# Last hidden values split in two parts, and VectorE's products and adds put ahead of weight splits in the small experts

## The reference, cut to what matters

```python
hn = rmsnorm(h, ffn_norm_g)
up = causal_dwconv(hn @ w_up, ffn_conv_w, ffn_conv_b)   # w_up: 2048 x 11264
val, gt = jnp.split(up, 2, axis=-1)
h = h + (jax.nn.silu(gt) * val) @ w_down                 # w_down: 5632 x 2048
x = rmsnorm(h, final_norm_g)                             # end of the first block
...
# second block: norm1 of x (shifted and scaled), attention, norm2, then 16 experts of width 512
def moe_ffn(h, router_w, router_bias, w_gate, w_up, w_down):
    aff = jax.nn.sigmoid(t @ router_w)
    # one of 4 groups of experts for each token, and 2 experts of that group
    ...
    # y = sum over chosen experts of  w_e * (silu(t @ w_gate[e]) * (t @ w_up[e])) @ w_down[e]
```

## Time and profile before

| | |
|---|---|
| median of 3 runs | 2907.25 us |
| the three runs | 2906.62, 2907.25, 2908.99 us |
| the profiled execution | 2910.48 us, its span 2907.6 us |
| TensorE busy in that span | 97% |
| VectorE, ScalarE busy | 76%, 52% |
| mean granted TensorE clock | 0.989 of 2.4 GHz |

### The profile page before, as it was taken

One profiled execution on the slowest core, in us unless ns is written; L12 is line 12 of the kernel. 1 busy time (PEld: TensorE's weight loads), 2 busy tenths in 40 slices (PEclk: granted clock), 3 DMA queues, 4 the chain that ended last, 5 costly groups with the idle time before them and its releaser, 6 DMA issues.

```text
span 2907.6 us, 45616 instructions
## 1 busy us (share of the span) xinstructions
PE 2827.7 (97%) x17842; PEld 2539.5 (87%) x17842; DVE 2197.8 (76%) x2740; ACT 1510.2 (52%) x1723; POOL 158.5 (5%) x228
## 2 busy tenths in 40 slices
PE   9999999999999999999999989999999999999998
PEld 8888888888888899999999989998989999977876
DVE  5644459999876899999999974655765778787786
ACT  5444564445554544444444454556545555556666
POOL 3000010000101000000000020111110000000001
PEclk9999999999999999999999999999999999999999
DMA  7445445555453978888888737444406777778885
GB/s 283 176 157 185 169 157 187 190 190 188 175 220 128 376 312 325 327 329 324 320 328 329 294 120 272 173 168 163 138 19 236 287 263 274 282 279 332 317 326 207
DMA packets 115678, 692.23 MB, mean 238 GB/s; under 512 B 14240, under 2 KB 27792, under 8 KB 34768
## 3 DMA queue, kind: packets, MB, share of 16 engines
q1 hardware_dynamic: 109952, 675.33, 61.5%
q10 hardware_dynamic: 4688, 11.01, 1.2%
q0 software_dynamic: 896, 3.93, 0.4%
HBM read 679.74 MB, written 10.49 MB: 237 GB/s over the span
## 4 chain that ended last, share of the span: by engine, by line
PE 84%; DVE 8%; ACT 4%; issue 2%; DMA 1%; SPq 0%; POOL 0%; DVEq 0%; POOLq 0%; ACTq 0%
PE psT L1310 22%; PE psT L1311 11%; PE psT L1297 6%; PE psT L1298 6%; PE psT L1299 6%; DVE w_lo L2092 4%; PE psT L1419 3%; PE psT L1887 2%; PE psT L1889 2%; PE psT L1888 2%; ACT w_hi L642 2%; PE psT L1898 2%; PE psT L1900 2%; PE psT L1899 2%; PE psT L1421 1%
## 5 line engine op out<-in xcount | busy, mean ns | idle before, releaser
L2092 DVE TENSOR_TENSOR w_lo<-raw,w_hi 128x2048 fp32r<-128x2048 f32 x532 | 1218.5, 2296 | 356.5 <-ACT w_hi L642 351.5
L642 ACT ACTIVATE w_hi<-raw 128x2048 fp32r<-128x2048 f32 x532 | 1013.2, 1910 | 405.4 <-PE psT L1299 130.8
L1310 PE MATMUL psT<-a_both,w_hi 128*128 128x512 f32 x3072 | 1084.2, 398 | 10.1 <-DVE pool L2453 2.9
L1311 PE MATMUL psT<-a_both,w_lo 128*128 128x256 f32 x3072 | 859.0, 280 | 0.0
L1310 PEld LDWEIGHTS psT<-a_both,w_hi 128*128 128x128 f32 x3072 | 577.4, 188 | 149.8 <-issue 8.9
L1311 PEld LDWEIGHTS psT<-a_both,w_lo 128*128 128x128 f32 x3072 | 579.9, 189 | 0.3
L1297 PE MATMUL psT<-a_both,w_hi 128*128 128x256 f32 x784 | 228.6, 292 | 7.7 <-DVE w_lo L2265 2.9
L1298 PE MATMUL psT<-a_both,w_hi 128*128 128x256 f32 x784 | 223.6, 285 | 0.0
L1299 PE MATMUL psT<-a_both,w_lo 128*128 128x256 f32 x784 | 223.6, 285 | 0.0
L2439 DVE CUSTOM_DVE_ANT_0 pool<-pool 128x2048 f32<-128x2048 f32 x96 | 219.2, 2284 | 5.2 <-DVE mod L2447 5.2
L1297 PE MATMUL psT<-h_hi,w_hi 128*128 128x256 f32 x768 | 219.1, 285 | 3.0 <-DVE h_lo L2479 1.7
(11 more groups left out here) (409 smaller groups left out, 4531.1 us busy)
## 6 DMA issues: line engine op xcount, KB each, us to landing
raw<-tiles_dram SPq DMA_DIRECT2D x532, 1024.0 KB, 5.3
pool<-ada_tiles_dram SPq DMA_DIRECT2D x96, 1024.0 KB, 5.0
bias_rows_dram<-pool ACTq DMA_DIRECT2D x1, 8192.0 KB, 56.2
pool<-bias_rows_dram SPq DMA_DIRECT2D x40, 128.0 KB, 4.6
pool<-bias_rows_dram SPq DMA_DIRECT2D x40, 64.0 KB, 4.6
pool<-mem_dram SPq DMA_DIRECT2D x4, 512.0 KB, 8.8
raw<-tiles_dram SPq DMA_DIRECT2D x8, 256.0 KB, 8.3
pool<-x_dram ACTq DMA_DIRECT2D x1, 2048.0 KB, 11.4
```

Source lines behind the costliest of these rows:

```text
L642: nc.scalar.activation(w_hi[:, t.k % SPL, :], raw[:, t.k % RAW, :], ACT.Copy).then_inc(hi_done, 1)
L1310: nc.tensor.matmul(dst.rearrange("p (h s) -> p h s", h=2), wh, a_both[:, :, a, :], start=first, stop=False)
L1311: return nc.tensor.matmul(dst[:, 0:S], wl, a_hi[:, a, :], start=False, stop=last)
L2092: nc.vector.tensor_tensor(w_lo[:, t.k % SPL, :], raw[:, t.k % RAW, :], w_hi[:, t.k % SPL, :].bitcast(F32), ALU.subtract).then_inc(lo_done, 1)
```

## The change

It has three parts. In the **feed-forward tail** the last of the ten loop rounds is written out on ScalarE and VectorE. In its last slot the first three chunks of the hidden values are split as soon as they exist, and the fourth by itself after the last pair; the VectorE split of tile 282 (the third of the last four), which stood in that slot, comes after the fourth chunk. TensorE runs the products of the first of the last four tiles in two parts, chunks 0 to 2 and then chunk 3, without filler ahead of them; the bias rows' product comes after that tile. On VectorE the bias rows' add goes behind the first `add_down`, the gain products of the third group go to the end with those of the fourth, and the split of tile 285 behind them. TensorE's product with the lane goes behind the last chunks 0 to 2.

In the **drained stages** (experts 7 and 11) `expert_hidden` moves from the drain into the last slot of up, ahead of the weight split there; for expert 7 ScalarE's copy of the lower rows moves ahead of its split likewise.

In **gate(9) and gate(13)** `expert_hidden` goes ahead of the first weight split, and the second round's four adds stand together behind the third split, instead of two behind the third and two behind the fourth.

```diff
@@ ScalarE, ffn_groups
-                with act.Fori(0, G1 - 1) as i:
+                def ffn_group(i, b8, last):
                     for n in range(12):
...
                         split(t + k + AHEAD)
+                        if last and n == 11:
+                            act.wait_ge(W["pairs_read"], 4 * G1 + 1)
+                            act.wait_ge(used, (b8 + 7).count())
+                            nc.scalar.activation(h_hi[:, 0:3, :], chunks(HF, 3), ACT.Copy)\
+                                .then_inc(W["last_hidden_hi"], 1)
                         if n // 4 != 1:
                             up_lower(t, k, i + 1, half)
...
+                with act.Fori(0, G1 - 2) as i:
+                    ffn_group(i, Tile(b + 8, i, 12, b + 8), False)
+                ffn_group(G1 - 2, Tile(b + 8 + 12 * (G1 - 2)), True)
                 up_silu(3, G1 - 1, 1)
-                hidden_hi(Tile(b + 12 * G1 - 5), G1 - 1)
+                act.wait_ge(W["pairs_read"], 4 * G1 + 2)
+                nc.scalar.activation(h_hi[:, 3, :], pool[:, HF + 3, :], ACT.Copy).then_inc(W["hidden_hi"], 1)
@@ ScalarE, experts
+                        if k == 3 and e in DRAINED and s == 3:
+                            up_lower_rows(e)
                         split(Tile(up_at(e) + k + AHEAD))
...
                     into = DRAINED[e]
-                    if s == 3:
-                        up_lower_rows(e)
@@ TensorE, ffn_groups
-                idle_products(8)
+                t = Tile(b + 12 * G1 - 4)
+                begin(t)
+                pe.wait_ge(W["last_hidden_lo"], 1)
+                for part in (range(3), range(3, 4)):
+                    if 3 in part:
+                        pe.wait_ge(W["hidden_lo"], G1)
+                    for n in range(4):
+                        for k in part:
+                            ...
+                            nc.tensor.matmul(dst, wh, h_hi[:, k, :], start=k == 0 and n % 2 == 0, stop=False)
+                            nc.tensor.matmul(dst, wh, h_lo[:, k, :], start=False, stop=False)
+                            last = nc.tensor.matmul(dst, wl, h_hi[:, k, :], start=False, stop=k == 3 and n % 2 == 1)
+                last.then_inc(used, 1)
                 pe.wait_ge(L["tables"], 48)
                 nc.tensor.matmul(psP[0:32, :], flat(Q2, 1)[0:32, 0:32], flat(Q2 + 1, 2)[0:32, :], start=True, stop=True)\
                     .then_inc(W["bias_rows"], 1)
-                idle_products(6)
-                pe.wait_ge(W["hidden_lo"], G1)
-                for k in range(4):
+                for k in range(1, 4):
                     down(Tile(b + 12 * G1 - 4 + k))
...
-                run_lane("final", FINAL_LANE, start=False)
+                wait(pe, W["variance_ready"], NORM_AT["final"])
                 for c in range(4):
+                    if c == 3:
+                        pe.wait_ge(W["lanes_added"], 3 * RUN.index("final") + 3)
+                        nc.tensor.matmul(psN, ones[:, :], pool[:, FINAL_LANE, :], start=False, stop=False)
                     run_last("final", c, US)
@@ VectorE, ffn_groups (the round is written out as on ScalarE)
-                            lo(t + n + AHEAD)
+                            if last and n == 11:
+                                dve.wait_ge(W["last_hidden_hi"], 1)
+                                nc.vector.tensor_tensor(h_lo[:, 0:3, :], chunks(HF, 3), h_hi[:, 0:3, :].bitcast(F32),
+                                                        ALU.subtract).then_inc(W["last_hidden_lo"], 1)
+                            else:
+                                lo(t + n + AHEAD)
...
-                hidden_lo(G1 - 1)
+                dve.wait_ge(W["hidden_hi"], G1)
+                nc.vector.tensor_tensor(h_lo[:, 3, :], pool[:, HF + 3, :], h_hi[:, 3, :].bitcast(F32), ALU.subtract)\
+                    .then_inc(W["hidden_lo"], 1)
+                lo(Tile(b + 12 * G1 - 5) + AHEAD)
+                ada_keep(ADA_EACH, G1 - 2)
...
                     if k < 3:
-                        lo(t + AHEAD)
+                        if k < 2:
+                            lo(t + AHEAD)
                         add_down(t + -k, k)
+                        if k == 0:
+                            bias_rows()
+                        if k == 2:
+                            continue
...
+                    for g in (2, 3) if k == 3 else (k,):
+                        ins = nc.vector.tensor_tensor(chunks(PRE + 4 * g, 4), chunks(H + 4 * g, 4), ...)
                 link(ins)
+                lo(Tile(b + 12 * G1 - 2) + AHEAD)
@@ VectorE, experts, stage gate
-                        if k == 0 and before == 0:
+                        early = before == 0 or e - 1 in SCATTERED_IN
+                        if k == 0 and before is not None and early:
                             expert_hidden(e - 1)
...
                         lo(Tile(gate_at(e) + k + AHEAD))
-                        if k == 0 and before:
+                        if k == 0 and before is not None and not early:
                             expert_hidden(e - 1)
-                        if k > 1 and e - 1 in SCATTERED_IN:
-                            round_add(SCATTERED_IN[e - 1], 1, range(2 * k - 4, 2 * k - 2))
+                        if k == 2 and e - 1 in SCATTERED_IN:
+                            round_add(SCATTERED_IN[e - 1], 1, range(4))
@@ VectorE, experts, stage up
+                        if k == 3 and e in DRAINED:
+                            expert_hidden(e)
                         lo(Tile(up_at(e) + k + AHEAD))
@@ VectorE, experts, stage drain
-                    expert_hidden(e)
```

More of the change, by code:

```diff
@@ L2494, in ffn_groups, with ffn_group @@
                 ada_keep(ADA_FIRST)
-                with dve.Fori(0, G1 - 1) as i:
-                    with step.loop(i, 9, G1 - 1):
-                        t = Tile(b + 8, i, 12)
+                def ffn_group(i, t, last):
                         for n in range(12):
```

34 lines of the change are left out of this document (23 added, 11 removed).

## The result

The changed kernel took 2886.86 us (median of 6 runs, 2883.53 to 2889.97) against 2908.12 for the kernel before in the same comparison (6 runs, 2901.89 to 2912.08). The ratio is 0.9923, with a 95% interval of 0.9913 to 0.9933, so the change takes off 22.4 us (19.5 to 25.3); the two medians themselves are 21.3 apart. The forecast was 2881 with a range of 2875 to 2892: side and range held, and the sum of 26.4 was 4.0 us too large and outside that interval. The profiled execution took 2887.1 us for a span of 2885.3, so span against span it is 22.3 shorter.

What follows compares the result with a forecast made beforehand. TensorE's waits and the slow clock behind them were taken to bound the kernel. The terms 7.7 + 4.1 + 0.8 + 7.5 + 6.3 = 26.4 us came off the median of 2907.25, giving 2881, range 2875 to 2892.

Steps and rivals of the forecast that it cites:

- What bounds the kernel: Whole kernel: TensorE carries 84% of the chain; time is won only where it stands still or runs slowly afterwards.
- Part 1a: Feed-forward tail, hidden values in two parts: second down tile starts at 1679.7 instead of 1684.6, 4.9 us won.
- Part 1b: Feed-forward tail, what is late next: fourth down tile waits 1.8 us; GpSimd's last group starts 5.3 us earlier.
- cross-sum: Check of the tail's total: 5.3 + 4.5 less 1.4 and 0.9, said to give 7.7 us within rounding.
- Part 1c: End of the norm: three products follow the lane instead of nine, 4.5 us won; VectorE and GpSimd alternate, root at 1707.5.
- lock rival: Tail: VectorE's three operations go in a row, so the tail gives 5.0 us, time 2884; chance 0.14.
- Part 2: Drained stages: expert 7's wait falls from 3.2 to 0.95, a second is 0.9, gain 4.1 us; expert 11 gains 0.8.
- clock rival: Drain 7: two waits of 0.9 close together still lower the clock, 2.8 us comes back, time 2884; chance 0.13.
- Part 3: Gates 9 and 13: shorter waits and no slow stretch behind them, gains of 7.5 and 6.3 us.
- transfers rival: Experts 8 to 15: without pauses, transfers at 353 GB/s bind and 24 us come back, time 2905; chance 0.06.
- signs that I would be wrong: ScalarE waiting for landings in a row, fourth down tile waiting over 2.4 us, or gates' down products still waiting for L2869.
- part 1: Whole feed-forward tail: root 7.7 us nearer to the last up tile, 34.9 instead of 42.6 behind it; bounds 5.0 to 9.5.

Runs made afterwards that it cites:

- split_only: Kernel before plus only the last hidden values and first down tile in 3 plus 1 parts, bias rows' product behind it; timed once, root 39.6 us behind last up tile.
- lane_back: Kernel before with the whole tail change, but TensorE's lane product ahead of the last four chunks as before; timed once, root 37.2 us behind last up tile.
- adds_first: Changed kernel with the tail's order pushed on: VectorE's second sum and gain products earlier, ScalarE's norm squares ahead of gain squares; 2888.78 us, ratio to before 0.9931.
- drains_only: Kernel before with only the drained stages' part of the change (experts 7 and 11); 2907.86 us, ratio 0.9989.
- early_only: Kernel before with only the hidden values' product ahead of VectorE's first split in gates 9 and 13; timed once, waits of 1.66 gone, those of 3.28 stayed.
- moe_only: Kernel before with only the drains and gates changed, feed-forward tail as before; 2897.86 us, ratio 0.9953.
- filler_only: Kernel before with 24 filler products of TensorE put into each of three waits of 3.2 to 3.3 us; no time given, clock 1.00 in those places.
- adds_only: Kernel before with only the four adds together behind the third split in gates 9 and 13; timed once, L2869 waits gone, those of 1.65 stayed.
- all_orders: Changed kernel with the tail's order pushed on, gate adds ahead of the third split, and a drain split moved behind the lower half; 2891.78 us, ratio to before 0.9933.
- tail_only: Kernel before with only the feed-forward tail's part of the change, experts as before; 2903.22 us, ratio 0.9969.

## Why the prediction was right, and where it was off

**What bounds the kernel**: right. All that TensorE got back were the waits listed in the earlier trace rows, the tail, and the clock.

**Part 1a, 4.9**: the down products start without a gap behind the last up tile, and the gap ahead of chunk 3 is 0.17 (0.35 said). The second down tile starts 7.2 behind the last up tile instead of 12.0, so 4.7 came. `split_only` gives 3.0 at the root for the edit alone, since GpSimd's group then ends last; the prediction didn't claim it alone.

**Part 1b**: the new wait ahead of the fourth down tile is 0.62, not 1.8. The term that I mis-sized is the chain from ScalarE's split of tile 284 to the second add. That add ends at 1695.6, 19.5 behind the last up tile, and I had it 20.4 behind (1693.05 less 1672.65). The wait is 1.2 shorter than said, and the tail gave 9.3 instead of 7.7, inside the bounds of 5.0 to 9.5. The rest of that 1.6, some 0.4, is VectorE's work in the last group, which the prediction ended at 34.9 and which ended at 33.3. The prediction's cross-sum for this part (5.3 + 4.5 less 1.4 and 0.9) makes 7.5 and not 7.7; its timeline carries the 7.7.

**Part 1c**: the alternation of VectorE and GpSimd came as said: GpSimd's adds took 1.59 and 1.59 beside the gain products and the split, where the earlier trace rows have 0.74 alone and 2.79 beside a split. The lane's place is worth 2.2 plus the clock (`lane_back`). The root starts when VectorE's split ends, as said.

Here the page that I had weighed, SBUF — State Buffer in the Trainium skill, section Who interferes with whom, agrees with the trace on the block itself: 1.59, 1.60 and 2.66 for an add of 0.74. The lock rival (5.0, all three in a row) didn't come in after, and in `adds_first`, with more two-input work of VectorE there, the two engines took turns as well; it lost because GpSimd got one add between two of VectorE's instructions.

**Part 2**: the first wait of drain 7 is 0.96 (0.95 said), the second 0.74 (0.9 said), clock 1.00, gain 4.1 as said; drain 11 gives 0.9 (0.8 said). The clock rival is out: two waits of 0.96 and 0.74 close together left it at 1.00, in all five executions that have them. Over 10 runs `drains_only` gives 3.2. With 1.6 of clock, the mean, in place of 2.8 the sum would be 3.7; the runs can't tell it from 4.9.

**Part 3**: 7.3 and 6.0 came for 7.5 and 6.3. The down products still wait 0.52 and 0.49 for the adds, where I had 0.1. The three waits of the sum went together, as argued; `early_only` shows that the product's place and the adds' place pay separately.

**Sum and median.** By its own steps, the profiled pair has 27.6 (9.3 + 4.1 + 0.9 + 7.3 + 6.0) against 26.4, so the steps are good. The median gained 22.4, and the step that failed is the one from the trace to the runs: "the waits are part of all runs, so I take the sum off the median". The waits are; their price in clock isn't. It was 8.8 in the sum and 5.5 as the mean over the executions seen, which is 3.3 of the 4.0 missing. This is an estimate from six or seven executions for each place: 27.6, less 2.8 for the clock (8.3 to 5.5) and less 2.6 for the waits on landings, is 22.2. The transfers rival has some truth as well. Landings in a row do occur, which was one of the signs that I would be wrong, but they cost TensorE 2.2 us in the profiled execution and not 24. The rate of 353 that I worked with the earlier trace rows is not the limit, since 384 and 424 were moved over stretches of about 30 us. That the transfers catch up in the drains, turns and scatters, where TensorE uses no new weights, fits the trace but was not tested.

The parts measured by themselves agree with this: 13.7 (8.7 to 18.3) for parts 2 and 3, where 18.7 was said, and 9.0 (4.4 to 13.7) for part 1, where 7.7 was.

## What to carry to other kernels

Where TensorE waits for a small result of an engine that also prepares weights, put the small result first and let the prepared tile use its slack; group the last small results so that they end with TensorE's own work. Price a wait by its length, and add the clock only as a mean over several executions: of one profile the slow stretch may be at its largest. When a chain over two engines that block each other is the goal, look at which of them the others wait for before moving more work next to it.

## What the runs showed of the hardware

- One and the same TensorE wait of 3.17 us was followed by 0, 1.6 or 2.6 us of lost time at the lower clock (six executions), and one of 3.28 by 0 to 2.6. In the tail and the small experts, up to the last wait on GpSimd, all waits of 1.80 or less left the clock at 1.00. One of 1.88 and one of 2.11 were followed by 3.4 us at the lower level, while one of 2.43 was not in four executions (`moe_only`, `filler_only`, `drains_only`, `adds_only`), nor one of 2.85 (`all_orders`) and one of 2.90 (`tail_only`).
- 12 products of ones, 0.23 us each, in waits of 3.2 and 3.3 kept the clock at 1.00: filler, well sized, gave 5.8 us (2.6 to 9.3) with nothing else changed.
- A GpSimd add of 256 columns took 0.74 alone, 1.6 beside a VectorE gain product and 2.65 to 2.79 beside a weight split; VectorE's split, 2.29 alone, took 2.7 to 3.4 when GpSimd was at work.
- The end of unchanged work moved by up to 9.4 us between executions (1672.3 to 1681.7 for the last up tile), more than most terms of the sum. Distances from a landmark in the same execution repeat far better: 33.3 three times for the tail, and waits to 0.01 us.
- The same 1 MB loads ran at 365 GB/s in one stretch of 32 us and at 424 in another of 30 us, with the DMA's share at 0.96 and 1.01.
